# Value projection of the forgetting attention: eight block products in rows, or seven block products with sums

## The reference

```
z  = hn @ ev_w_in                      # hn: 256 x 1024 normalised tokens
xr, yr = z[:, 0:512], z[:, 512:1024]   # inputs of the LRU
q, k, v = z[:, 1024:1536], z[:, 1536:2048], z[:, 2048:2560]
# LRU: convolution over 4 tokens, two gates, a scan over the tokens, times gelu(yr)
# fox: softmax(q k' / 8 + cumulative log-gate differences, causal) @ v
h  = h + concat(lru, fox) @ ev_w_out
```

## Time and profile before

| | before |
|---|---|
| median of 3 runs | 2733.9 us |
| profiled execution | 2737.4 us |
| its span | 2735.6 us |
| PE busy | 98% of the span, 20744 matmul records |
| DVE busy | 63% |
| ACT busy | 17% |
| POOL busy | 4%, 134 instructions |
| chain that ended last | PE 82%, DVE 9%, DMA 7%, ACT 1% |
| granted clock of PE, mean | 0.997 |

### The profile page before, as it was taken

How to read it: one execution, slowest core, us unless ns; L and a number is a source line. 1 busy time by engine, 2 the same in 40 slices (tenths; PEclk the granted TensorE clock), 3 DMA queues, 4 the chain that set the end, 5 groups by cost and what they waited for, 6 DMA issues and landing times.

```text
span 2735.6 us, 48510 instructions
## 1 busy us (share of the span) xinstructions
PE 2673.2 (98%) x20744; PEld 2067.6 (76%) x20744; DVE 1730.1 (63%) x3026; ACT 475.1 (17%) x939; POOL 102.2 (4%) x134
## 2 busy tenths in 40 slices
PE   9999999999999999999999999999999999999998
PEld 6789887776688879777776787756777777777765
DVE  3654464776355437477655674546778778778776
ACT  2220212101222121200142111320111111111111
POOL 0011300000001220000000000000000000000000
PEclk9999999999999999999999999999999999999999
DMA  6321443444233243444343443339999999999995
GB/s 270 120 110 72 177 152 121 175 185 155 108 131 124 78 172 121 170 170 173 128 154 124 185 154 141 123 136 416 421 386 420 416 388 419 423 396 407 418 411 237
DMA packets 59294, 621.29 MB, mean 227 GB/s; under 512 B 6721, under 2 KB 7105, under 8 KB 10945
## 3 DMA queue, kind: packets, MB, share of 16 engines
q1 hardware_dynamic: 55008, 602.25, 55.4%
q0 software_dynamic: 2720, 13.52, 1.2%
q10 hardware_dynamic: 1344, 2.36, 0.2%
HBM read 614.70 MB, written 3.41 MB: 226 GB/s over the span
## 4 chain that ended last, share of the span: by engine, by line
PE 82%; DVE 9%; DMA 7%; ACT 1%; issue 1%; SPq 0%; DVEq 0%; ACTq 0%
PE ps L1390 10%; PE ps L1782 9%; PE ps L821 9%; PE ps L1402 8%; PE ps L1243 7%; PE ps L1802 6%; PE ps L863 5%; PE ps L1817 4%; PE ps L1221 4%; DMA slabA<-in_od_exp_w 3%; DMA fbT<-in_od_exp_w 2%; PE ps L1857 2%; PE ps L802 2%; PE ps L1255 2%; PE ps L1368 1%; PE ps L908 1%
## 5 line engine op out<-in xcount | busy, mean ns | idle before, releaser
L1802 PE MATMUL ps<-fbT,work 128*64 128x256 f32 x1792 | 207.4, 384 | 7.1 <-DMA fbT<-in_od_exp_w 6.9
L1243 PE MATMUL ps<-hT,slabA 128*128 128x256 f32 x832 | 188.9, 380 | 1.1 <-ACT work L2130 1.1
L1802 PEld LDWEIGHTS ps<-fbT,work 128*64 128x64 f32 x1792 | 124.5, 138 | 75.2 <-DMA fbT<-in_od_exp_w 10.0
L1243 PEld LDWEIGHTS ps<-hT,slabA 128*128 128x128 f32 x832 | 155.7, 190 | 23.4 <-ACT work L2130 1.9
L1782 PE MATMUL ps<-prm,hT 128*64 128x128 f32 x2592 | 161.6, 273 | 8.4 <-DVE resets L3432 8.3
L2456 DVE TENSOR_TENSOR work<-work 128x256 f32<-128x256 f32 (+2 forms) x207 | 85.3, 412 | 128.7 <-ACT work L2102 98.3
L821 PE MATMUL ps<-hT,slabA 128*128 128x256 f32 x736 | 163.4, 381 | 0.0
L1782 PEld LDWEIGHTS ps<-prm,hT 128*64 128x64 f32 x2592 | 145.1, 136 | 20.6 <-DVE resets L3432 11.8
L1390 PEld LDWEIGHTS ps<-work 128*128 128x128 f32 x1152 | 139.5, 192 | 21.5 <-issue 21.0
L821 PEld LDWEIGHTS ps<-hT,slabA 128*128 128x128 f32 x736 | 138.3, 190 | 20.5 <-issue 2.5
L1390 PE MATMUL ps<-work 128*128 128x128 f32 x1152 | 143.9, 275 | 0.1
(11 more groups left out here) (533 smaller groups left out, 4675.7 us busy)
## 6 DMA issues: line engine op xcount, KB each, us to landing
slabA<-in_od_exp_w SPq DMA_DIRECT2D x56, 2048.0 KB, 12.9
fbT<-in_od_exp_w SPq DMA_DIRECT2D x56, 2048.0 KB, 10.6
slabB<-in_od_exp_w SPq DMA_DIRECT2D x56, 1024.0 KB, 12.3
fbT<-in_od_exp_w SPq DMA_DIRECT2D x56, 1024.0 KB, 13.3
slabA<-in_w_in SPq DMA_DIRECT2D x24, 2048.0 KB, 8.2
slabA<-in_mlp_w SPq DMA_DIRECT2D x16, 2048.0 KB, 9.3
slabB<-in_mlp_w SPq DMA_DIRECT2D x32, 1024.0 KB, 4.8
slabA<-in_ev_ffn_w SPq DMA_DIRECT2D x11, 2048.0 KB, 7.7
```

The lines of the kernel that those rows point to most:

```text
L1243: last = mm(ps[:, b, 0:T], side["gates"][:, k, c % 4 * P:(c % 4 + 1) * P], hT[:, k, :], start=(k == 0), stop=(k == KD - 1))
L1802: last = mm(ps[SMALL * j:SMALL * (j + 1), 1, 0:2 * P].rearrange("p (w n) -> p w n", w=2), xs[:, k, :], v[:, k, :, j * P:(j + 1) * P], star ...
```

## The change

The product of v is cut into 2 x 2 blocks: the tokens b into halves of the 1024 inner columns and halves of the tokens, the slab a into the same halves of the inner dimension and halves of 256 columns. In place of eight block products there are seven, four of which have sums of blocks as a factor, or as both.

- POOL makes the sums. `fox_sums` first makes four sums of token blocks (128 x 512 each), behind `lru_rows`, and then, when slab v has landed, four sums of weight blocks (128 x 1024 each). It stands in POOL's program ahead of the two loads of `gainrow`.
- PE computes the seven products in four parts, in the order 0, 2, 1, 3 (`rows_unit`, which `gla_unit` now calls too). Parts 2, 1 and 3 wait for POOL's sums. Each part is a bank of two products of 256 columns; part 3 has one.
- ACT copies four banks out into `fox_products`, three of 512 columns and one of 256.
- DVE joins them with four additions (`rows_join`), behind the first `fox_weights`. PE waits for that ahead of the first `fox_values`.
- SP releases slab v after four groups, not two.

```diff
--- before.py
+++ after.py
@@ -552,6 +552,10 @@
         def cross_PT(t):
             return U(13 + 2 * t)
 
+        fox_token_sums, fox_products = quarters(U(0, 2)), U(8, 2, size=7 * T).rearrange("p (c n) -> p c n", c=7)
+        fox_pair = U(12, size=2 * T).rearrange("p (q n) -> p q n", q=2)
+        fox_weight_sums = [m.rearrange("p (k n) -> p k n", k=4) for m in (fbT[:, UNIT:2 * UNIT], fbT[:, 7 * UNIT:8 * UNIT], U(14), U(15))]
+        even_slabs = DEPTH * 33
         FK = 104
         fq, fk = (fbT[:, 2048 * i:2048 * (i + 1)].rearrange("p (h t) -> p h t", h=8) for i in (1, 2))
         fox_groups = [(t, hg) for t in range(NT) for hg in range(2)]
@@ -690,7 +694,7 @@
                 linear(a["xa_wo"][l], D, rows)
                 ffn_steps(FF1 // STEP, False, a["mlp_w1"][l], a["mlp_w2"][l], ("rows_psum", 2))
             sums = (None, ("sum_psum", 2))
-            for i, n in enumerate((2, 3, 4, 4, 2)):
+            for i, n in enumerate((2, 3, 4, 4, 4)):
                 ringA.load(sp, [cols(a["ev_w_in_2"], EVEN_SLABS, 512 * i)], groups(n))
                 if i == 1:
                     ringB.load(sp, [cols(a["ev_w_in_2"], EVEN_SLABS, EVEN_SLABS[0][0])], ("few_taken", 1))
@@ -780,8 +784,30 @@
                         first = False
                         pool.dma_start(gainrow[:, :], row(a[n][l], P)).then_inc(sem("gainrow_loaded"), up("gainrow_loaded", 16))
 
+                def fox_sums():
+
+                    def pool_sum(o, i, j, op, done="fox_sums"):
+                        nc.gpsimd.tensor_tensor(o, i, j, op).then_inc(sem(done), up(done))
+                        pool.wait_ge(sem(done), at(done))
+                    pool.wait_ge(sem("lru_rows"), due("pool", "lru_rows"))
+                    b, s = hT.rearrange("p (h k) t -> p h k t", h=2), fox_token_sums
+                    b11, b12, b21, b22 = b[:, 0, :, 0:P], b[:, 0, :, P:T], b[:, 1, :, 0:P], b[:, 1, :, P:T]
+                    pool_sum(s[:, 0], b12, b11, ALU.subtract, "side_product")
+                    pool_sum(s[:, 1], b22, s[:, 0], ALU.subtract, "side_product")
+                    pool_sum(s[:, 2], b22, b12, ALU.subtract, "side_product")
+                    pool_sum(s[:, 3], b21, s[:, 1], ALU.subtract, "side_product")
+                    n = even_slabs + 4
+                    pool.wait_ge(sem(f"slabA_full{n % 2}"), 16 * (n // 2 + 1))
+                    w, ws = kview(ringA.bufs[n % 2], 512), fox_weight_sums
+                    a11, a12, a21, a22 = w[:, 0:4, 0:T], w[:, 4:8, 0:T], w[:, 0:4, T:2 * T], w[:, 4:8, T:2 * T]
+                    pool_sum(ws[0], a21, a22, ALU.add)
+                    pool_sum(ws[1], ws[0], a11, ALU.subtract)
+                    pool_sum(ws[2], a11, a21, ALU.subtract)
+                    pool_sum(ws[3], a12, ws[1], ALU.subtract)
+
                 pool.wait_ge(sem("nsa_done"), due("pool", "nsa_done", DEPTH))
                 pool.dma_start(fbT[:, 0:1024], a["lru_gate_w"]).then_inc(sem("lru_gate_loaded"), up("lru_gate_loaded", 16))
+                fox_sums()
                 for src in (a["od_head_norm_2"][0], a["norm_final_2"]):
                     pool.wait_ge(sem("gainrow_used"), due("pool", "gainrow_used"))
                     pool.dma_start(gainrow[:, :], row(src, P)).then_inc(sem("gainrow_loaded"), up("gainrow_loaded", 16))
@@ -861,6 +887,21 @@
                         for k in range(4):
                             one, two = (rhs, lhs) if turned else (lhs, rhs)
                             last = mm(ps[:, g, c * P:(c + 1) * P], one[:, k, :], two[:, k, :], start=(k == 0), stop=(k == 3))
+                    last.then_inc(sem("proj_ready"), up("proj_ready"))
+
+            def rows_unit(slab, ws, ts_, parts, summed, needed):
+
+                w, b = kview(slab, 512), hT
+                a11, a12, a22 = w[:, 0:4, 0:T], w[:, 4:8, 0:T], w[:, 4:8, T:2 * T]
+                b11, b21, b22 = b[:, 0:4, 0:P], b[:, 4:8, 0:P], b[:, 4:8, P:T]
+                factors = ((b11, a11), (b21, a12), (ts_[:, 2], ws[2]), (ts_[:, 1], ws[1]), (ts_[:, 0], ws[0]), (ts_[:, 3], a22), (b22, ws[3]))
+                for part in parts:
+                    g = next_bank()
+                    if part in needed:
+                        pe.wait_ge(sem(summed), due("pe", summed, needed[part]))
+                    for j, (lhs, rhs) in enumerate(factors[2 * part:2 * part + 2]):
+                        for k in range(4):
+                            last = mm(ps[:, g, j * T:(j + 1) * T], lhs[:, k, :], rhs[:, k, :], start=(k == 0), stop=(k == 3))
                     last.then_inc(sem("proj_ready"), up("proj_ready"))
 
             def chT(slab, n, c0, width, dst=0):
@@ -1543,9 +1584,8 @@
             s = ringA.take(pe)
             for j in range(4):
                 group([chT(s, 512, P * j, P)])
-            s = ringA.take(pe)
-            for t in range(NT):
-                group([rowsof(s, 512, 0, 512, t)])
+            assert ringA.taken == even_slabs + 4
+            rows_unit(ringA.take(pe), fox_weight_sums, fox_token_sums, (0, 2, 1, 3), "fox_sums", {2: 1, 1: 2, 3: 1})
             fv = fbT[:, 6144:7168].rearrange("p (n c) -> p n c", n=NT)
 
             def fox_scores(g):
@@ -1597,6 +1637,7 @@
             pe.wait_ge(sem("fox_max"), due("pe", "fox_max", 2))
             fox_scores(2)
             out_rows(0, 1, range(KD // 2))
+            pe.wait_ge(sem("unit_taken"), due("pe", "unit_taken"))
             fox_values(0)
             fox_turn(1)
             pe.wait_ge(sem("fox_max"), due("pe", "fox_max"))
@@ -1644,18 +1685,7 @@
 
                 if parts[0] == 0:
                     side["slab"] = ringA.take(pe)
...
+                rows_unit(side["slab"], gla_weight_sums(u), gla_token_sums, parts, "sums_ready", {1: 1})
             gla_unit(0, range(4))
             gla_unit(1, range(4))
             pe.wait_ge(sem("gla_in_sbuf"), due("pe", "gla_in_sbuf"))
@@ -2285,9 +2315,11 @@
             root(U(7))
             for i in range(2, 4):
                 two_heads(fk[0:HD], 2 * i, take())
-            for t in range(NT):
-                nc.scalar.activation(fv[:, t, :], take(), ACT.Copy).then_inc(sem("proj_free"), up("proj_free"))
+            for part in (0, 2, 1, 3):
+                n = min(2, 7 - 2 * part)
+                nc.scalar.activation(fox_products[:, 2 * part:2 * part + n, :], take()[:, 0:n * T].rearrange("p (c n) -> p c n", c=n), ACT.Copy).then_inc(sem("proj_free"), up("proj_free"))
                 act.wait_ge(sem("proj_free"), at("proj_free"))
+            units_out.append(count_of("proj_free").posted)
             nc.scalar.activation(stat[:, 60:61], stat[:, 60:61], ACT.Copy).then_inc(sem("even_inputs"), up("even_inputs"))
             act.wait_ge(sem("even_inputs"), at("even_inputs"))
 
@@ -2359,7 +2391,7 @@
 
             def gla_products_in(u, parts):
 
-                if u and parts[0] == 0:
+                if parts[0] == 0:
                     act.wait_ge(sem("unit_taken"), due("act", "unit_taken"))
                 for part in parts:
                     n = min(2, 7 - 2 * part)
@@ -2628,6 +2660,17 @@
                 add(pair_of, p[:, 2:5:2, :], d[:, b + 9:b + 10, :].broadcast_to([P, 2, P]))
                 add(d[:, b + 1:b + 9:7, :], pair_of, p[:, 5:7, :])
                 v.tensor_tensor(d[:, b + 9, :], pair_of[:, 0, :], p[:, 4, :], ALU.add).then_inc(sem("unit_taken"), up("unit_taken"))
+                dve.wait_ge(sem("unit_taken"), at("unit_taken"))
+
+            def rows_join(p, dst, b, pair):
+
+                n = dst.shape[2] // T + 1
+                d = dst.rearrange("p t c -> p (t c)").rearrange("p (q n) -> p q n", n=T)
+                dve.wait_ge(sem("proj_free"), units_out.pop(0))
+                add(d[:, b:b + n + 1:n, :], p[:, 1:4:2, :], p[:, 0:1, :].broadcast_to([P, 2, T]))
+                add(pair, p[:, 2:5:2, :], d[:, b + n:b + n + 1, :].broadcast_to([P, 2, T]))
+                add(d[:, b + 1:b + n:n - 2, :], pair, p[:, 5:7, :])
+                v.tensor_tensor(d[:, b + n, :], pair[:, 0, :], p[:, 4, :], ALU.add).then_inc(sem("unit_taken"), up("unit_taken"))
                 dve.wait_ge(sem("unit_taken"), at("unit_taken"))
 
             def ffn_products(steps, gated):
@@ -3178,6 +3221,7 @@
             fox_max(0)
             fox_max(1)
             fox_weights(0)
+            rows_join(fox_products, fbT[:, 6144:7168].rearrange("p (n c) -> p n c", n=NT), 0, fox_pair)
             dve.wait_ge(sem("fox_turned"), due("dve", "fox_turned"))
             fox_max(2)
             fox_weights(1)
@@ -3205,14 +3249,7 @@
 
             def gla_join(u):
 
...
+                rows_join(gla_products, gla_g if u == 2 else gla_v, 2 * (u % 2), gla_pair)
             token_block_sums(gla_token_sums, hT)
             gla_sums(0)
             dve.wait_ge(sem("gla_in_psum"), due("dve", "gla_in_psum"))
```

## The result

| | before | after |
|---|---|---|
| median of 8 runs | 2732.99 us (2731.35 to 2735.35) | 2742.59 us (2741.57 to 2744.36) |
| ratio after / before | | 1.0034, 95% interval 1.0024 to 1.0043 |
| profiled execution | 2737.4 us | 2742.3 us |
| span | 2735.6 us | 2740.5 us |
| POOL busy | 102.2 us | 119.7 us |

The account below looks back on a forecast made before the run. PE was taken as the bound, busy 98% of the span and 82% of the chain. Lateness of 6.7 us and 2.9 for the clock made 9.6; on profiled 2737.4 that is 2747.0, less 3.5 gives 2743.5 us, range 2737 to 2748.

Parts of the forecast that it names:

- The products and the end: PE's value projection: products gain 1.65 us and the 0.21 us idle ahead of the scores goes, together 1.85 us.
- POOL's length: POOL's weight sums of 1024 columns: 2.46 us each, 2.32 of it work, with bounds 2.29 and 2.88.
- the bound from 0.72 times four: Upper bound for one POOL weight sum: 2.88 us, if all of a 256-column operation's time grows with the columns.
- The turns: POOL's weight sums beside DVE's LRU chain: the engines alternate, each waiting out the other's whole operation; DVE 7.9 us late.
- rival 3: POOL against DVE: DVE wins every contest, PE waits for the sums instead; 4.6 us slower, 2738.5 us, chance 0.06.
- The bank: PE ahead of part 2 waits 8.6 us for ACT to free the bank of `two_heads(fk, 4)`; v done 6.9 us late.
- The clock: PE's records behind the long wait run at a lowered clock: 2.9 us more, bounds 0 and 8.6.
- Rival 1: PE behind its wait: the clock stays up, so only 6.7 us slower, 2740.6 us; chance 0.17.
- The token sums: POOL's four token sums hold up DVE's convolution by at most 4.7 us, hidden by its wait for ACT; cost nothing.
- The join: DVE's additions behind the first weights: 2.6 us, hidden by its wait for the scores but for 0.1 us.
- The base: From profile to median: profiled 2737.4 us with the loss is 2747.0, the median 3.5 us lower, 2743.5.
- The sum: Whole kernel: 6.7 us of lateness and 2.9 us for the clock make 9.6 us slower.

Follow-up runs that it names:

- v ahead of k: Changed kernel with slab v loaded and multiplied before slab k, sums waiting for `fox_exp_in`: 2731.43 us, ratio 0.9996 to the kernel before; with sums on DVE 2731.71 us, 0.9994.
- quarter sums: Changed kernel with POOL's weight sums over 256 columns instead of 1024, PE taking plain weight blocks: 2733.67 us, ratio 1.0002 to the kernel before.
- sums alone: Kernel before plus POOL's eight sums, which nothing reads; v's second group waits for them: 2741.59 us, ratio 1.0029 to the kernel before.
- PE is kept busy: Changed kernel with 18 products of 256 columns added on PE ahead of part 2, into an idle bank: 2740.19 us, ratio 1.0023 to the kernel before.

## Why the prediction was right

- **The products and the end.** Where the clock is up, eight records take 1.73 us, 0.216 each, and there is no idle ahead of the scores: both as worked out. With v ahead of k all 56 take 12.09 us (1399.57 to 1411.66). It is the only gain, and it shows once the sums stand elsewhere (1.46 us, with what the last copy of k costs already off it).
- **POOL's length.** 2.35 us alone, against 2.46 taken; the work itself, behind DVE's end at 1407.95, is 2.22 us (1406.95 and 3.22 is 1410.17), against 2.32. Scaling the held part of POOL's own row was right; the bound from 0.72 times four was far off.
- **The turns.** Sum 1, la times sp8, sum 2, iu times xc and so on, in the order written down, which rules out rival 3 (DVE wins every contest). DVE was 7.6 us late, against 7.9. The quarter sums and the sums alone show that this, and not the products, is the loss.
- **The bank.** PE waited 8.15 us, against 8.6, for the copy named. Of the 0.45 us between them 0.25 is DVE's smaller delay, and most of the rest the end of part 0, which the profile puts 3.62 us behind its start where the prediction took 3.45. ACT's copy ended 3.25 us behind DVE's `root_in` in both kernels.
- **The clock.** 24 records took 7.78 us (1425.12 to 1432.90) instead of 5.17: 2.6 us, against 2.9, and 2.5 are given back where PE is kept busy. Rival 1 (the clock stays up) is out by this.
- **The token sums** held DVE up by 3.7 us (its idle is 5.91 us instead of 9.60), under the 4.7 allowed, and hidden as said. **The join** is hidden but for the 0.1 us named.
- **The base.** The step "profiled 2737.4, and 3.5 off for the median" was right by its result only. The profiled execution after is 2742.3, at its own median: the profiles differ by 4.9 us, the medians by 9.6. From the first product of v to the scores, the stretch grew by 9.0 us in the profiles (14.97 to 24.02). But in the profile before part 0 began 0.6 us later, and 3.4 us more went by in stages that no edit touches: from the seven-product unit of the later layer to the first product of the experts 118.77 us against 116.64, with 1.39 us of it a wait for a slab, and from there to PE's last products 883.53 against 882.24. In the nine kernels of the experiments these two stretches vary from 115.86 to 118.29 and from 881.55 to 885.35 us. So the 3.5 us were scatter of one execution, and not a cost of profiling.
- **The sum.** The forecast was 9.6 us from 6.7 and 2.9; the traces show 9.0, about 6.4 and 2.6. That the medians differ by 9.6 as well, to the tenth, is luck: the interval of their ratio reaches from 6.6 to 11.8 us. The mechanism does not rest on it.

In "sums alone" the wait of 4.56 us and the 2.3 us of the slow records make 6.9 us; the medians say 8.2. The 1.3 us between them lie within the interval of the ratio and are not placed.

## What to carry to other kernels

Before work is handed to POOL, look at what DVE does in the same microseconds. Here, where both read SBUF, each of four operations of DVE met one of POOL's (2.2 us of work) and ended 1.5 to 2.0 us later by it, more than the 1.2 us that DVE needs to make such a sum itself. Ask which wait a late engine reaches first and which stands behind it: here a bank that ACT frees, then `lru_done`, and taking the first away gave half. Place such sums where the other engine waits, add the clock to the price of a wait of PE (2.3 to 2.9 us behind waits of 4.6 to 8.2 us here), and don't offset a profile against a median by the difference of one execution.

## What was not expected of the hardware

- DVE's operations on 8 partitions are held about as long as those on 128: a scan of 256 columns takes 2.35 us, where it takes 0.68 without POOL beside it, and a tensor_scalar 2.26 where it takes 0.28 (the two kernels with v ahead of k, with the sums on POOL and on DVE). The tensor_scalar of 128x1024 in the changed kernel takes 2.73 where it takes 0.69.
- POOL's memset of 128 x 1024, 0.95 us, and DVE's two-input operations pass each other without a hold.
- The clock fell behind two short waits of PE, 1.68 and 2.88 us with 3.7 us of work between them, while it stayed up behind a single one of 1.73 us in the kernel with the quarter sums.
